# TensorE's two loops written out: groups 1 to 3 of the pooling layer and heads 1 to 3 of the GLA layer

## The reference

```python
for li in range(2):
    mod = silu(c) @ ada_w[li] + ada_b[li]
    shift, scale, gate = split(mod, 3)
    h = rmsnorm(x, norm_g[li]) * (1 + scale) + shift
    y = pool_branch(h, ...) if li == 0 else gla_branch(h, ...)
    x = x + gate * y
return rmsnorm(x, final_g), new states
# pool_branch: u, z = split(h @ w_in, 2); mixed = (windowed means of u - u) @ w_grp (4 groups)
#              y = (mixed * scale * silu(z)) @ w_out
# gla_branch:  q, k, v, z, gl = split(h @ w_in); 4 heads, chunks of 32 tokens,
#              o = masked (q k) v + q S, S updated from chunk to chunk;
#              y = (rms-normed o * silu(z)) @ w_out
```

## Time and profile before

| | us |
|---|---|
| median of 3 runs | 1675.4 |
| lowest, highest | 1672.11, 1679.82 |
| the profiled execution | 1674.2 |
| its span | 1672.5 |
| TensorE busy | 1620.5 |
| VectorE, ScalarE, GpSimd busy | 824.4, 466.6, 395.5 |

### The profile page before, as it was taken

How to read it: one execution, slowest core, us unless ns; L and a number is a source line. 1 busy time by engine, 2 the same in 40 slices (tenths; PEclk the granted TensorE clock), 3 DMA queues, 4 the chain that set the end, 5 groups by cost and what they waited for, 6 DMA issues and landing times.

```text
span 1672.5 us, 25329 instructions
## 1 busy us (share of the span) xinstructions
PE 1620.5 (97%) x9827; PEld 1504.6 (90%) x9827; DVE 824.4 (49%) x1263; ACT 466.6 (28%) x977; POOL 395.5 (24%) x392
## 2 busy tenths in 40 slices
PE   6899999999999999998999999999999999999996
PEld 5799999999999999997788998889988989879896
DVE  5653549443944475457324562245612356223475
ACT  5421112111212011125325413154130541224423
POOL 3221212211211212112314122142130322213310
PEclk8999999999999999997999999999999999999999
DMA  9512221221122212210202212022120221201312
GB/s 332 184 55 77 66 67 41 84 73 42 55 76 64 68 54 66 72 32 27 63 17 73 82 43 73 13 70 89 40 65 12 64 94 40 64 25 39 107 38 107
DMA packets 137554, 115.18 MB, mean 69 GB/s; under 512 B 6013, under 2 KB 120281, under 8 KB 137442
## 3 DMA queue, kind: packets, MB, share of 16 engines
q1 hardware_dynamic: 135616, 112.87, 21.9%
q10 hardware_dynamic: 1834, 0.74, 0.2%
HBM read 99.05 MB, written 15.00 MB: 68 GB/s over the span
## 4 chain that ended last, share of the span: by engine, by line
PE 92%; DVE 3%; ACT 1%; issue 1%; DMA 1%; SPq 1%; POOL 1%; ACTq 0%; DVEq 0%; POOLq 0%
PE psA L556 39%; PE psB L556 28%; PE psB L1814 8%; PE psA L1814 4%; PE psB L1870 2%; PE psB L1887 2%; PE psX L1852 2%; PE psB L1878 1%; PE psX L1907 1%; DVE a_hi L644 1%; PE psB L1919 1%; DVE y_rows L1616 1%; PE psX L1730 1%; POOL h_lo L506 1%; ACT h_hi L517 1%
## 5 line engine op out<-in xcount | busy, mean ns | idle before, releaser
L344 POOL TENSOR_TENSOR w_lo<-stage,w_hi 128x1024 fp32r<-128x1024 f32 x100 | 249.6, 2496 | 859.2 <-ACT w_hi L339 859.2
L339 ACT ACTIVATE w_hi<-stage 128x1024 fp32r<-128x1024 f32 x100 | 107.0, 1070 | 434.6 <-PE psB L556 297.5
L556 PE MATMUL psA<-h_hi,w_hi 128*128 128x362 f32 (+1 forms) x864 | 212.8, 352 | 11.6 <-POOL h_lo L506 6.4
L556 PE MATMUL psA<-h_lo,w_hi 128*128 128x362 f32 (+1 forms) x864 | 195.5, 332 | 4.9 <-issue 4.9
L556 PE MATMUL psA<-h_hi,w_lo 128*128 128x362 f32 (+1 forms) x864 | 194.7, 331 | 0.0
L556 PEld LDWEIGHTS psA<-h_hi,w_hi 128*128 128x128 f32 x864 | 152.4, 192 | 36.5 <-issue 23.7
L556 PEld LDWEIGHTS psA<-h_lo,w_hi 128*128 128x128 f32 x864 | 153.1, 192 | 5.2 <-issue 5.2
L556 PEld LDWEIGHTS psA<-h_hi,w_lo 128*128 128x128 f32 x864 | 153.1, 192 | 0.0
L556 PE MATMUL psA<-a_hi,w_hi 128*128 128x362 f32 (+1 forms) x480 | 109.4, 333 | 2.6 <-DVEq L650 1.3
L556 PE MATMUL psB<-h_hi,w_hi 128*128 128x362 f32 (+1 forms) x480 | 109.8, 331 | 0.0
L556 PE MATMUL psB<-h_lo,w_hi 128*128 128x362 f32 (+1 forms) x480 | 108.0, 328 | 0.0
(11 more groups left out here) (347 smaller groups left out, 2823.8 us busy)
## 6 DMA issues: line engine op xcount, KB each, us to landing
stage<-in_gla_w_in SPq DMA_DIRECT2D x40, 512.0 KB, 3.8
stage<-in_pool_w_in SPq DMA_DIRECT2D x32, 512.0 KB, 4.2
ada_stage<-in_ada_w SPq DMA_DIRECT2D x24, 512.0 KB, 3.7
ada<-in_ada_w SPq DMA_DIRECT2D x16, 512.0 KB, 8.6
stage<-in_pool_w_out SPq DMA_DIRECT2D x16, 512.0 KB, 3.4
v<-in_state_gla SPq DMA_DIRECT2D x32, 256.0 KB, 2.6
out_new_gla_sample<-v SPq DMA_DIRECT2D x32, 256.0 KB, 2.0
stage<-in_gla_w_out SPq DMA_DIRECT2D x16, 512.0 KB, 3.5
```

Source lines behind the costliest of these rows:

```text
L339: nc.scalar.activation(slot_hi(plan, j), stage[:, j % 2, :], ACT.Copy).then_inc(lay.hi_done, 1)
L344: nc.gpsimd.tensor_tensor(slot_lo(plan, j), stage[:, j % 2, :], slot_hi(plan, j).bitcast(f32), ALU.subtract).then_inc(lay.lo_done, 1)
L556: last = nc.tensor.matmul(ps[u][:, t, 0:width], weight(w[:, p, :], k), a[:, k, n0:n0 + width], start=(k == 0 and pas == 0), stop=(k == kt ...
```

## The change

The two loops of TensorE become Python loops: the builder writes the body three times, with `g` a constant. The other engines' programs are unchanged.

```diff
             pool_products(0, True)
-            with pe.Fori(1, NG) as g:
+            for g in range(1, NG):
                 pool_products(g, False)
...
-            head(0, True)
-            with pe.Fori(1, NG) as g:
-                head(g, False)
+            for g in range(NG):
+                head(g, g == 0)
```

## The result

The changed kernel takes 1665.18 us (median of 10 runs, 1662.63 to 1668.92), the kernel before in the same comparison 1676.1 us (median of 10, 1671.81 to 1680.31). The ratio is 0.9933, with a 95% interval of 0.9919 to 0.9946: 11.2 us off, between 9.1 and 13.6. The forecast was 1662.0 in a range of 1657 to 1668, faster; the time lies in the range, 3.2 us above the forecast.

What follows compares the result with a forecast made beforehand. The prediction took TensorE to bound the kernel; removing its jumps back would save 0.93 + 1.10 + 5.45 + 5.68 = 13.16 us, from the median 1675.4 - 13.2 = 1662.2, forecast as 1662, range 1657 to 1668.

Steps and rivals of the forecast that it cites:

- What bounds the kernel, and where the time lies: TensorE, busy 1620.5 of 1672.5 us, bounds the kernel; rounds 2 and 3 of both layers, reached by jumping back, are longer.
- the second gap: GLA layer, three matmuls into heads 2 and 3: a step of 3.23 us in head 2 where 0.49 is usual.
- The pooling term: Pooling layer: without two jumps back, groups 2 and 3 lose 0.93 and 1.10 us, sum 2.03 us.
- The GLA term: GLA layer: without two jumps back, heads 2 and 3 lose 5.45 and 5.68 us, sum 11.13, at least 10.4.
- the 0.37 us: Unexplained extra from head 2's value rows to its end, counted into the gain; the low bound leaves out 2 x 0.37.
- Registers, entries and code size at nothing: TensorE: dropping register instructions and two loop entries gains nothing; growing from 3,355 to 6,267 program rows costs 0.
- Another engine's slack: Rival: another engine's hidden jump back comes out, giving 1667.6 us; chance 0.07. Against it stood slack of 12 us.
- only the first gap goes: Rival: the second gap comes from code falling on a block and stays; gain 3.8 us, time 1671.6; chance 0.10 including no change.
- the first gap: Longer step right at a round's start after a jump back: 0.85 and 1.03 us in pooling, 0.76 in GLA head 2.

## Why the prediction was right, and where its sizes were off

**What bounds the kernel, and where the time lies**: right. TensorE's own stream was the chain, the four rounds behind a jump back were the longer ones, and with the jump gone they are as long as the rounds without. The forecast didn't need to know what the second gap was: the round that is reached without a jump was its measure.

**The pooling term** (0.93 + 1.10): 0.94 and 1.12 in the profile after. In the third profile of before the two cost 1.23 and 1.40, so the mean of three profiles is 2.2 us, not 2.03.

**The GLA term** (11.13, at least 10.4): the mechanism was right, its size was off. It measured 11.13 in the first profile and 9.01 and 8.09 in the others, mean 9.4. I worked it out from a single execution and gave it a low bound from the 0.37 us alone, as though the gaps themselves were fixed. They are not: the block came 2.68 us after the target's first matmul in the second and third profiles and 3.22 to 3.23 in the first, and the clock falls behind the gap or doesn't. With both terms taken from three profiles the sum is 11.6 us (13.16, 11.04 and 10.72). The prediction had no term for the norm; the stretch from the last group to head 1 is 0.8 us longer in the changed kernel (mean of four profiles, 245.27, against 244.46 of three), which leaves 10.8, and the comparison measured 11.2 (by the medians 10.9). The 3.2 us by which the median missed the forecast are 13.2 - 10.9 = 2.3 from the gain, of which 1.6 is the draw of the first profile; 0.7 since the kernel before ran at 1676.1 and not at the 1675.4 of the runs shown; and 0.2 from rounding.

**The 0.37 us**: wrong to count in. Straight code has it too, in one profile in one head and in the next in another, and the second and third profiles of before have it in none of heads 0 to 3. What makes it is open.

**Registers, entries and code size at nothing**: right, and the loops that run once show it for the first two by themselves. Straight code cost nothing at a block's border: no idle time put down to "issue" in groups 1 to 3 or in any head. I had expected about 85 packets of code and 78 came: the two extra blocks of each jump back are gone.

**Another engine's slack**: right. No row that opens a round waits for another engine, and writing out the other four moved nothing that the runs can tell from no change.

**The second gap.** I could not say what it was and gave "only the first gap goes" 0.10. Its argument, that the code falls on a block, was true; its conclusion was not. The gap needs both, the block's end close behind the target and the jump that has emptied what was read ahead. That is why head 1, with the same code at the same place, never had it. The rule of the Trainium skill (Runtime: NRT & Kernel Launch, section Instruction fetch mechanics), that a taken branch whose target isn't at hand forces a fetch before execution goes on, holds for the first gap: the packet with the target's block starts 0.94 us after the jump at head 2. The runs add that the block behind the target's is asked for only once the target is reached, and comes 2.67 to 3.23 us after its first row, less the work in hand. The first gap is short because matmuls queued ahead cover most of the 3.41 us; behind it nothing is queued any more, so the second fetch is paid nearly whole.

## What to carry to other kernels

On a bound engine look at the first rows of a hardware loop's second round, against those of its first: idle time put down to "issue" there was the jump back, about 1 us here (0.9 to 1.4), and 3 to 6 us where the target stands a few instructions before the end of a code block. Writing the loop out took all of it; where the code must stay a loop, a few dummy instructions ahead of it, placed where the engine waits anyway, gave 6.4 of the 11.2 us. A gap of this kind is a draw, so take its size from several profiles before it goes into a sum.

## What the runs showed of the hardware

- After a jump back the block behind the target's came between 2.67 us (group 2 in the run with 214 increments) and 3.23 us (head 2 in the first profile of before) after the target's first row, in loops of either layer.
- An idle stretch of 1.91 us was followed by full clock (1.00 over the next 4 us, head 2 of the third profile of before), one of 1.92 us in the next head of the same profile by 0.57. The 2.19 us of the run with 214 increments were followed by 0.66 in head 2 and by 1.00 in head 3. The 36 small matmuls of the norm took 4.85 to 6.65 us in four profiles of one kernel, as the clock fell later or sooner. What decides the moment is open.
- Semaphore increments in a row on TensorE took 0.15 us each (214 at its start, 240 ahead of the GLA layer). Ahead of the GLA layer sixteen of them, and even 42, lay hidden: the stretch from the last group to head 1 was 244.87 and 243.86 us, where the three profiles of before have 243.85 to 245.00.
- A loop that is entered and left without a taken jump back cost nothing on TensorE, register counts included: groups took 174.13 to 174.14 us and heads 212.96 to 212.97, written out 174.12 to 174.15 and 212.92 to 212.96 (without the 0.34 us).
